# A single-core three-block network: the first projection behind two norms taken as a pair of chunks by token, the attention mask added first, the compression in one piece, PSUM banks turned

## The reference

```python
# block 1, two layers; each: x = layer_norm(a*x + mixer(x)); x = layer_norm(a*x + sqrelu(x@w1)@w2)
# mixer of layer 1: sparse attention and pooling
s_w = einsum('bghqd,bgkd->bghqk', q, k_w);  p_w = masked_softmax(s_w, wmask)
kc  = gelu(blocks_of(k_cmp) @ cmp_w1 + b1) @ cmp_w2        # compression, also for v
# mixer of layer 2: gated linear attention on h = x @ c_w_in, split into q, k, v, r, a
# block 2: proj = x @ w_in, split into q, k, v, z, a, b, uv, gate_dn, gate_sgu
u, v = split(gelu(uv), 2); v = layer_norm_2(v)             # spatial gating unit
y = sigmoid(gate_dn) * (delta_rule(q,k,v) * silu(z)) @ w_dn_out + sigmoid(gate_sgu) * sgu @ w_sgu_out
x = layer_norm_2(h + y @ w_out); x = layer_norm_2(x + moe(x))   # 16 experts
```

## Time and profile before

| | us |
|---|---|
| three runs | 1258.65, 1259.85, 1264.12 |
| median | 1259.85 |
| profiled execution | 1259.07 |
| its span | 1257.3 |

### The profile page before, as it was taken

The page is one execution under the profiler, slowest core; times in us unless marked ns, Lnnn a source line. Parts: engine busy times, 40 slices in busy tenths (PEclk is TensorE's granted clock), DMA queues, the critical chain, the costliest instruction groups (busy, mean ns, idle before and its releaser), DMA issues.

```text
span 1257.3 us, 19376 instructions
## 1 busy us (share of the span) xinstructions
PE 1236.1 (98%) x8278; PEld 1126.9 (90%) x8278; DVE 809.5 (64%) x961; ACT 610.2 (49%) x721; POOL 166.3 (13%) x137
## 2 busy tenths in 40 slices
PE   8999999999999999999999999999999999999997
PEld 8978999998999899999899989898888999999996
DVE  6477855558665875655798338843877775555556
ACT  4565443335636534343476457645845633333332
POOL 8500400000500040000320400040000040000000
PEclk9999999999999999999999999999999999999999
DMA  9804575653642475566675335442754565556550
GB/s 256 203 35 134 190 235 180 199 184 120 226 146 81 165 254 181 189 201 132 154 151 134 101 101 134 135 101 68 251 201 134 168 233 171 193 176 199 173 197 34
DMA packets 140023, 204.93 MB, mean 163 GB/s; under 512 B 13603, under 2 KB 101394, under 8 KB 139938
## 3 DMA queue, kind: packets, MB, share of 16 engines
q1 hardware_dynamic: 137714, 195.80, 50.9%
q0 software_dynamic: 2224, 7.90, 1.9%
HBM read 202.63 MB, written 1.05 MB: 162 GB/s over the span
## 4 chain that ended last, share of the span: by engine, by line
PE 80%; DVE 9%; ACT 4%; DMA 3%; SPq 2%; issue 2%; DVEq 0%; ACTq 0%
PE PS L387 33%; PE PS L392 17%; PE PS L551 10%; PE PS L521 4%; DVE w_lo L1204 2%; ACT w_hi L1817 2%; PE PS L1027 2%; PE PS L1040 1%; DVE st L1233 1%; SPq L2405 1%; DVE res L1231 1%; DMA ring<-in_w_in 1%; PE PS L489 1%; PE PS L458 1%; DMA ring<-in_a_w_out 1%
## 5 line engine op out<-in xcount | busy, mean ns | idle before, releaser
L1204 DVE TENSOR_TENSOR w_lo<-ring,w_hi 128x2048 fp32r<-128x2048 f32 x182 | 432.4, 2382 | 208.7 <-ACT w_hi L1817 208.5
L1817 ACT ACTIVATE w_hi<-ring 128x2048 fp32r<-128x2048 f32 x182 | 347.9, 1914 | 246.5 <-PE PS L392 202.5
L387 PE MATMUL PS<-x_hi,w_hi 128*128 128x256 f32 x1104 | 268.2, 283 | 0.0
L387 PE MATMUL PS<-x_lo,w_hi 128*128 128x256 f32 x1104 | 267.8, 283 | 0.0
L1829 ACT ACTIVATE AR<-PS 128x512 f32<-128x512 f32 x154 | 87.3, 599 | 262.1 <-PE PS L392 169.7
L387 PEld LDWEIGHTS PS<-x_hi,w_hi 128*128 128x128 f32 x1104 | 211.5, 192 | 2.8 <-issue 1.1
L387 PEld LDWEIGHTS PS<-x_lo,w_hi 128*128 128x128 f32 x1104 | 211.7, 192 | 1.7
L387 PE MATMUL PS<-w_hi,o_hi 128*128 128x512 f32 x384 | 150.3, 391 | 0.8 <-DVE o_lo L1461 0.8
L387 PE MATMUL PS<-w_hi,o_lo 128*128 128x512 f32 x384 | 150.0, 391 | 0.0
L392 PE MATMUL PS<-x_hi,w_lo 128*128 128x256 f32 x1120 | 146.1, 283 | 0.2 <-DVE w_lo L1337 0.2
L392 PEld LDWEIGHTS PS<-x_hi,w_lo 128*128 128x128 f32 x1120 | 139.5, 192 | 0.4 <-DVE w_lo L1337 0.4
(11 more groups left out here) (421 smaller groups left out, 1867.6 us busy)
## 6 DMA issues: line engine op xcount, KB each, us to landing
ring<-in_mlp_w SPq DMA_DIRECT2D x64, 1024.0 KB, 5.2
ring<-in_w_in SPq DMA_DIRECT2D x32, 1024.0 KB, 7.6
ring<-in_expert_w_gate SPq DMA_DIRECT2D x16, 1024.0 KB, 5.4
ring<-in_expert_w_up SPq DMA_DIRECT2D x16, 1024.0 KB, 5.3
ring<-in_expert_w_down SPq DMA_DIRECT2D x16, 1024.0 KB, 4.9
ring<-in_c_w_in SPq DMA_DIRECT2D x12, 1024.0 KB, 5.2
ring<-in_a_w_in SPq DMA_DIRECT2D x4, 1024.0 KB, 9.0
ring<-in_c_w_out SPq DMA_DIRECT2D x4, 1024.0 KB, 4.9
```

The source lines that it names most:

```text
L387: mm(out, a, b, start=first and i == 0, stop=False, skip_group_check=True)
L1204: v.tensor_tensor(w_lo[:, m % PARTS], ring[:, index[split[m]] % RING], w_hi[:, m % PARTS].bitcast(F32), ALU.subtract)\
L1817: a(w_hi[:, m % PARTS], ring[:, index[split[m]] % RING], ACT.Copy).then_inc(S("hi_split"), 1)
```

## The change

Four things. (1) Chunks gv 0 and 1 and uv 4 and 5 are `paired` instead of `cols`, stand side by side in the stream, and are both done behind their norm by a new generator `pair_with_norm`: 48 products of 512 columns, ordered after the pieces of x as they come; `by_token(("gv", 1))` and the 16 fill steps of ("uv", 5) go. (2) In `scores` the mask product comes first and once a unit. (3) The compression's 16 products come in one piece, after six steps of `triples`. (4) Banks are taken in another order at three places, and ACT copies `av` after one w_hi rounding instead of two.

```diff
--- before.py
+++ after.py
@@ -248,17 +248,16 @@
         cwi = A["c_w_in"][0]
-        cols("gv", cwi, 1024, 1)
+        paired("gv", cwi, 1024, 2)
         cols("gq", cwi, 0, 2)
         cols("gk", cwi, 512, 2)
-        cols("gv", cwi, 1024 + W, 1, 1)
         paired("gv", cwi, 1024 + 2 * W, 2, 2)
...
         UV = 3072 + 1024 + 16
-        cols("uv", wi, UV + 1024, 1, 4)
+        paired("uv", wi, UV + 1024, 2, 4)
         for hb in range(2):
@@ -267,7 +266,6 @@
                 paired("gs", wi, UV + 3072, 4)
-                cols("uv", wi, UV + 1024 + W, 1, 5)
                 paired("uv", wi, UV + 1024 + 2 * W, 2, 6)
@@ -500,6 +498,54 @@
                 filled.append(chunk)
+            def pair_with_norm(pre, i, l):
+                names = (pre, i), (pre, i + 1)
+                n = take(names[0])
+                ps = [claim(pe, names[t], t) for t in range(TT)]
+                def part(t, b, x_, w, first=False, last=False):
+                    for k in range(KT // 2):
+                        if x_ is x_hi and k == 2 and (t, b) != (0, 1):
+                            pe.wait_ge(S("x_hi_vector"), 3 * l + 2 * t + b + (t == 0))
+                        ins = mm(ps[t], x_[:, KT // 2 * b + k, t * P:(t + 1) * P], w[:, k, :], start=first and k == 0,
+                                 stop=last and k == KT // 2 - 1, skip_group_check=True)
+                    return ins
+                def rounded(t, b):
+                    if (t, b) == (0, 1):
+                        pe.wait_ge(S("x_hi"), l + 1)
+                    else:
+                        pe.wait_ge(S("x_hi_direct"), 3 * l + 2 * t + b + (t == 0))
+                def low(t, b, w):
+                    pe.wait_ge(S("x_split"), 4 * (l + 1) + 2 * t + b + 1)
+                    return part(t, b, x_lo, w)
+                wh, wl = (w[:, n, :].rearrange("p (k n) -> p k n", k=KT // 2) for w in (w_hi, w_lo))
+                rounded(0, 0)
+                part(0, 0, x_hi, wh, first=True)
+                part(0, 0, x_hi, wl)
+                low(0, 0, wh)
+                yield
+                n = take_high(names[1])
+                wh_, wl_ = (w[:, n, :].rearrange("p (k n) -> p k n", k=KT // 2) for w in (w_hi, w_lo))
+                rounded(0, 1)
+                part(0, 1, x_hi, wh_)
+                low(0, 1, wh_)
+                rounded(1, 0)
+                part(1, 0, x_hi, wh, first=True)
+                part(1, 0, x_hi, wl)
+                spent(low(1, 0, wh), names[0])
+                rounded(1, 1)
+                part(1, 1, x_hi, wh_)
+                low(1, 1, wh_)
+                take_low(names[1])
+                for t in range(TT):
+                    close(part(t, 1, x_hi, wl_, last=True), names[t], names[1] if t else None)
+                    filled.append(names[t])
@@ -633,7 +679,7 @@
                 if ln is not None:
-                    steps = with_norm(then, 0, ln)
+                    steps = pair_with_norm(*then, ln) if then[0] in ("gv", "uv") else with_norm(then, 0, ln)
                     advance(steps, 1)
@@ -712,12 +758,12 @@
             steps = triples(("au", 1), nxt())
+            advance(steps, 6)
             arrived(pe, "cmp_w1")
...
             for k in range(16):
-                advance(steps, 1)
                 ins = mm(ps[:, 0:60], w[:, k, :], a_kb[:, :, k].rearrange("p v g c -> p v (g c)"), start=(k == 0), stop=(k == 15))
@@ -758,11 +804,12 @@
                 ps = claim(pe, ("s", u), nxt(2, 8))
+                mm(ps.rearrange("p (h k) -> p h k", h=nh)[:, :, t * P:nk], identb[:], maskb[:].unsqueeze(1).broadcast_to([P, nh, P]),
+                   start=True, stop=False, skip_group_check=True)
                 for i in range(nh):
                     head = (h * nh + i)
-                    mm(ps[:, i * nk:(i + 1) * nk], a_q[:, head, t * P:(t + 1) * P], a_kk[:, g, a, 0:nk],
-                       start=True, stop=False, skip_group_check=True)
-                    ins = mm(ps[:, i * nk + t * P:(i + 1) * nk], identb[:], maskb[:], start=False, stop=True, skip_group_check=True)
+                    ins = mm(ps[:, i * nk:(i + 1) * nk], a_q[:, head, t * P:(t + 1) * P], a_kk[:, g, a, 0:nk],
+                             start=False, stop=True, skip_group_check=True)
                 close(ins, ("s", u))
@@ -845,6 +892,7 @@
             advance(steps)
+            turn[0] += 1
             by_feature(("gq", 0))
@@ -864,7 +912,6 @@
                 close(ins, ("gb", t))
-            by_token(("gv", 1))
             advance(token_pair("gv", 2, (nxt(), nxt())))
@@ -955,7 +1002,8 @@
                 if hb == 0:
-                    steps = pair("q", 0, (nxt(), nxt()))
+                    turn[0] += 2
+                    steps = pair("q", 0, (0, 2))
                     advance(steps, 16)
@@ -995,7 +1043,7 @@
                 else:
-                    fill = in_turn([(token_pair, "gs", i, (6, 7)) for i in (0, 2)] + [(triples, ("uv", 5), 6, True), (token_pair, "uv", 6, (7, 6))])
+                    fill = in_turn([(token_pair, "gs", i, (6, 7)) for i in (0, 2)] + [(token_pair, "uv", 6, (6, 7))])
                 advance(fill, 6)
@@ -1918,7 +1966,7 @@
             a(a_sc[:, :, :, 0:NCMP], a_sc[:, :, :, 0:NCMP], ACT.Exp).then_inc(S("c_exp"), 1)
-            ps = bank("av")
+            ps = bank("av", 1)
             for t in range(TT):
@@ -1966,7 +2014,8 @@
-            copy(("gv", 0), c_v[:, :, 0:W], lambda ps: ps.rearrange("p (t n) -> p t n", t=TT))
+            for t in range(TT):
+                copy(("gv", t), c_v[:, t, 0:BANK])
             for j in range(2):
@@ -1983,7 +2032,6 @@
                 evacuated(a(flat(c_en[:, t]), ps, ACT.Exp, scale=-1.0 / 16), ("gb", t))
-            copy(("gv", 1), c_v[:, :, W:2 * W], lambda ps: ps.rearrange("p (t n) -> p t n", t=TT))
             for t in range(TT):
@@ -2024,8 +2072,6 @@
                         copy(chunk, u_v[:, i % 2, BANK:])
-                    elif what == "uv" and i >= 4:
-                        copy(chunk, u_v[:, :, (i - 4) * W:(i - 3) * W], lambda ps: ps.rearrange("p (t n) -> p t n", t=TT))
                     elif what in ("z", "gd", "gs"):
@@ -2070,7 +2116,8 @@
-            copy(("uv", 4), u_v[:, :, 0:W], lambda ps: ps.rearrange("p (t n) -> p t n", t=TT))
+            for t in range(TT):
+                copy(("uv", 4 + t), u_v[:, t, 0:BANK])
             split_ahead(pieces_for["ab"], 1)
@@ -2158,7 +2205,7 @@
                 read(("uv", 4 + i))
-                g = u_v[:, :, i * W:(i + 1) * W] if i < 2 else u_v[:, i % 2, BANK:]
+                g = u_v[:, i % 2, i // 2 * BANK:(i // 2 + 1) * BANK]
                 a(g, g, ACT.Gelu).then_inc(S("v_gelu"), 1)
```

## The result

The changed kernel took 1253.24 us, the median of five runs (1251.03 to 1253.51), beside 1258.73 for the kernel before (five runs, 1258.44 to 1264.12). The ratio is 0.9942 with an interval of 0.9927 to 0.9958: 0.6% faster, some 7 us, with bounds of 5 and 9. The two medians lie only 5.5 apart; the means of the five runs lie 7.25 apart, as the ratio says. The forecast was 1253.0. The profiled execution took 1253.51, its span is 1251.7, against 1259.07 and 1257.3.

The account below looks back on a forecast made before the run. PE's products were taken as the bound, 80% of the chain that ended last. Norm 1 −1.2, norm 3 −1.3 and −1.8, attention −2.6, compression and banks 0 summed to −6.9 us, giving 1253.0, range 1249.7 to 1257.8.

Parts of the forecast that it names:

- Norm 1: Pairing gv 0 and 1 behind norm 1: −1.2 us, 0.6 from wider products and 0.6 from shorter waits.
- Norm 3: Pairing uv 4 and 5 behind norm 3: −1.3 us, and −1.8 more from the first w_in chunk landing earlier.
- Its cause: Norm 3's slow transfer: first touch of 1024 far-apart rows, so a paired chunk of 512 rows lands in 8 to 10 us.
- the rival that it stood behind (1254.8): First w_in chunk at norm 3 lands no earlier, so only −5.1 us in all; chance 0.22.
- Attention: Earlier av copy and one mask product per unit: −2.6 us, bounds −0.4 and −2.9.
- The step that DVE's chain carries the gain through: In the attention, DVE's softmax starts as much earlier, so the 2.2 us gained ahead of the transposes carry through.
- Compression: The 16 products in one piece: 0, difference within 0.1 us, upper bound +0.15.
- Banks: Taking banks in another order at three places: 0, or at most +0.6 us if one waits for a copy.
- for w_lo in the pair: Rival: behind the norms, the pair waits for DVE at its last eight products; −3.9 us, 1256.0; chance 0.09.
- for DVE in the attention past 1.5: Rival: the attention's removed wait returns as a wait for DVE; −4.7 us, 1255.2; chance 0.07.
- 512-column products under 0.227: Rival: 512-column products run faster in the pairs than in token_pair; −17.1 us, 1242.8; chance 0.02.
- the clock behind the compression: Rival: granted clock falls from 2.4 to 1.2 GHz behind the one-piece compression; +17 us, 1277; chance 0.03.

Follow-up runs that it names:

- Run 4: Changed kernel with chunks gv 0 and 1 fetched and multiplied as before: 1.31 us longer from compression to end than the changed kernel; median 1253.18.
- run 9: Changed kernel with uv 4 and 5 and the banks of pair q 0 as before: 2.05 us longer from compression to end than the changed kernel; median 1255.27.
- run 2: Changed kernel with uv 4 and 5 fetched in 1 KB pieces of 512 rows, products unchanged: 0.05 us longer from compression to end; median 1251.61.
- run 5: Kernel before, with uv 4 fetched by two issues of 512 rows instead of one of 1024: landing 15.1 us, 1259.12 in one run.
- run 3: Kernel before, plus a small transfer reading 16 bytes of each of uv 4's 1024 rows two chunks ahead: median 1260.5, ratio 0.9993.
- run 6: Changed kernel with ACT's copy of av behind two w_hi roundings again: 1.59 us longer from compression to end; median 1253.87.
- run 10: Kernel before, with only ACT's copy of av moved ahead of its second w_hi rounding: 1.58 us shorter from compression to end; median 1261.26, ratio 1.0000.
- run 8: Changed kernel with DVE's first w_lo split of the attention behind the second unit's weighting, not the first's: 0.57 us shorter from compression to end; median 1251.28.
- run 12: Changed kernel with DVE's first attention split behind the second unit's weighting and the compression strewn in as before: 0.59 us shorter from compression to end; median 1252.02.
- run 11: Changed kernel with the compression strewn in and the banks of pair q 0 as before: 1.01 us longer from compression to end; median 1252.67.
- run 1: Changed kernel with uv 4 and 5 as before: 4.12 us longer from compression to end than the changed kernel; median 1255.74.

## Why the prediction was right

**The sum.** −6.9 was forecast, −7.26 measured in the long stretch, about −7.3 by the ratio, −5.5 by the medians. The median, 1253.24, came 0.2 from the forecast; the kernel before measured 1258.73 in this comparison and 1260.0 to 1261.1 in the later ones, so the nearness of the two absolute numbers is partly luck. Two of the larger terms, the transfer and the wait in the attention, are moreover those of the one execution that was read; both come out at their upper end because the same execution is the base of the 7.26. The upper bound of the range, 1257.8, leaves out the compression's 0.15 that it names; its sum is 1257.9.

**Norm 1**: −1.2 forecast, −1.3 to −1.4. The step that laid the new order on the old arrival times gave 12.98 for the pair; it took 12.9, and of its waits the one that was named stood, 1.0 long. Run 4 has this term alone, 1.3.

**Norm 3**: −1.3 for the pair, 1.3 by run 9; −1.8 for the transfer, and the trace of the change has its moments 1.9 earlier, counted from the 512-column products ahead. But that term is one of an execution, not of the kernel: in six profiles with 1024 rows ACT waited 1.78, 0.48, 0.80, 1.92, 0.66 and 2.07. On average it is 1.3. The forecast took the one profile at its word, and the mean would have made the sum −6.4.

**Its cause** was half right. Half the rows took half the time, whether a piece had 1 or 2 KB (run 2), and two issues instead of one changed nothing (run 5). But the count of rows is not enough: the touch took 7.2 us for as many rows (run 3), and uv 5, as tall and cut as finely, took 8.9 behind chunks from the same rows. "The first touch" fits the last and fell in the form in which it was tested, 16 bytes read 9 us ahead (run 3). The Trainium skill, "DMA: Bandwidth & Descriptors", section "Specifications", puts the least transfer for line rate at 512 B; the pieces of 1 KB were at 60 to 108 GB/s and at 350 within one chunk, so for these rows the rule is not enough, and the rival that it stood behind (1254.8) fell.

**Attention**: −2.6 forecast, −2.86. The copy is worth 1.5 to 1.9 (runs 6 and 10), forecast with 1.8; with the chunk on time, as in run 3, PE waited 0.84 for it and it would be worth about 0.9, an estimate from that wait. The masks are 0.9 instead of 0.7: a unit of four heads went from 1.34 to 1.11, where 1.17 was forecast. The step that DVE's chain carries the gain through did not hold in full: DVE's wait grew by 0.4, behind a split that runs 8 and 12 move for another 0.6. The larger gain of the masks covered it.

**Compression**: 0 forecast, bound +0.15, measured +0.09: slower, if by little, and strewn in again it is 9.23 (runs 11 and 12).

**Banks**: 0 forecast, and wrong as a price of its own: at q 0 the turn saves the pair 0.8. It was put at nothing since no wait stands there in the old order; but the pair holds other banks, and longer. Within the sum it came out right, since what was forecast was the order with the turn.

**Delta rule's end**: nothing forecast, −0.1. The rivals' waits (for w_lo in the pair, for DVE in the attention past 1.5, 512-column products under 0.227, the clock behind the compression) did not come: four products of 512 columns are 0.91 apart, and three float32r products behind the compression 0.36.

## What to carry to other kernels

A wait ended by a copy may be due not to that copy but to the order of the engine that makes it: one rounding moved behind one copy gave 1.5 to 1.9 us. A projection that starts on pieces of a norm gained 1.3 us at each of two norms when it was built from products as wide as the bank, laid out on the arrival times that the old trace shows, with the products that need the last weight at the end. Count a wait on a transfer over several executions before it goes into a sum, and ask of every pair of banks who holds them in the new order.

## What was not expected of the hardware

As the first chunk of their matrix, 1024 rows at a pitch of 32.8 KB took 13.7 to 15.3 us to land in six traces, 512 rows 7.6 to 8.3 us with twice the bytes in each; a second column half of the same rows, right behind, came three to four times as fast at its peak, and a chunk of 1024 rows behind two others from the same rows took 8.9; 16 bytes of each of the 1024 rows took 7.2 us and helped nothing 9 us later. How long a row stays fast, and why, is open.

PE's first 5 to 20 products of 256 columns run at a distance of 0.21 in some executions and 0.12 in others, at a clock column of full speed. In the changed kernel it is worth 1.7 us, a quarter of what this change gives, and a comparison of two spans must take it out.

A wait of 1.8 us of PE inside the delta rule (run 3) was followed by two microseconds at a mean granted clock of 0.66 and two at 0.50, the lower level. It came in one of fourteen profiles; a wait of 1.2 at the same place (run 1) had no such slice. Ahead of both, by 45 us, a DVE operation of 128x16 took 2.42 and 1.36 us instead of 0.17, until a GpSimd operation beside it had ended.
